# Hybrid encoder trunk on one core: norm-weight waits at first use, one key decay issued earlier, two low parts moved to GpSimd

## The reference, cut to what matters

```
h = rmsnorm(x, norm_mix_pre);  z = h @ w_in
cq, ckv, kr, hq, hff, hfb, hi, hg = split(z)          # 256, 128, 32, then 5 x 512
q  = rmsnorm(cq, q_norm) @ w_uq ; kv = rmsnorm(ckv, kv_norm) @ w_ukv    # 8 heads, 64 + 32 rotary
a  = rmsnorm(softmax attention(q, k, v), att_out_norm)
r  = rmsnorm(gated recurrence forward + backward, hg_out_norm) * silu(hg)   # 4 heads of 128
x  = x + rmsnorm([a, r] @ w_o);  MLP with squared relu;  per-layer embedding gate
```

## Time and profile before

| | |
|---|---|
| median of 3 runs | 1367.94 us |
| the profiled execution | 1365.97 us, of it 1364.2 us from the first to the last instruction |
| mean granted TensorE clock | 0.996 |
| TensorE matmul busy | 1327.0 us, 97% |
| VectorE, ScalarE, GpSimd busy | 877.4, 671.6, 677.9 us |

### The profile page before, as it was taken

The page is one execution under the profiler, slowest core; times in us unless marked ns, Lnnn a source line. Parts: engine busy times, 40 slices in busy tenths (PEclk is TensorE's granted clock), DMA queues, the critical chain, the costliest instruction groups (busy, mean ns, idle before and its releaser), DMA issues.

```text
span 1364.2 us, 22084 instructions
## 1 busy us (share of the span) xinstructions
PE 1327.0 (97%) x8300; PEld 1082.5 (79%) x8300; DVE 877.4 (64%) x1180; ACT 671.6 (49%) x1245; POOL 677.9 (50%) x538
## 2 busy tenths in 40 slices
PE   6999999999989999999999999999999999999997
PEld 5887878877857777888888888888888888878886
DVE  6126656555876775166755565657899888895384
ACT  6333333344458775356755545454544444445452
POOL 4364546365547744455577777775100553003490
PEclk9999999999999999999999999999999999999999
DMA  6231110112240004443533434337667734674351
GB/s 208 70 77 35 30 48 25 36 41 63 55 101 2 1 1 139 170 133 123 194 115 114 126 108 124 111 121 240 231 218 245 245 104 140 236 249 139 87 186 69
DMA packets 138265, 162.28 MB, mean 119 GB/s; under 512 B 16688, under 2 KB 82224, under 8 KB 138160
## 3 DMA queue, kind: packets, MB, share of 16 engines
q1 hardware_dynamic: 138160, 160.87, 37.8%
HBM read 139.86 MB, written 18.87 MB: 116 GB/s over the span
## 4 chain that ended last, share of the span: by engine, by line
PE 78%; DVE 6%; issue 3%; ACT 2%; POOL 2%; DMA 1%; SPq 0%; DVEq 0%; POOLq 0%; ACTq 0%
PE ps L51 23%; PE ps L53 23%; PE ps L52 22%; PE ps L1889 2%; PE ps L1051 2%; PE ps L1930 2%; PE ps L1701 2%; PE ps L1084 1%; DVE op_low L2367 1%; PE ps L998 1%; DVE wy_low L2373 1%; DVE w_sum L2344 0%; DMA gain<-in_att_out_norm 0%; POOL k_low L1718 0%; DMA raw_more<-keep_e 0%
## 5 line engine op out<-in xcount | busy, mean ns | idle before, releaser
L1601 POOL TENSOR_TENSOR wy_low<-w_raw,wy_high 128x512 fp32r<-128x512 f32 x107 | 159.2, 1490 | 179.0 <-ACT wy_high L1544 178.9
L51 PE MATMUL ps<-wy_high,op_high 128*128 128x512 f32 x448 | 175.0, 391 | 1.3 <-DVE wy_low L2373 0.9
L52 PE MATMUL ps<-wy_low,op_high 128*128 128x512 f32 x448 | 174.3, 389 | 0.0
L53 PE MATMUL ps<-wy_high,op_low 128*128 128x512 f32 x448 | 174.3, 389 | 0.0
L1544 ACT ACTIVATE wy_high<-w_raw 128x512 fp32r<-128x512 f32 x118 | 74.4, 631 | 153.7 <-PE ps L53 149.5
L400 POOL TENSOR_TENSOR wx_low<-w_raw,wx_high 128x512 fp32r<-128x512 f32 x62 | 82.8, 1340 | 115.6 <-ACT wx_high L530 115.6
L1601 POOL TENSOR_TENSOR wy_low<-t_sum,wy_high 128x512 fp32r<-128x512 f32 x64 | 89.4, 1397 | 53.9 <-ACT wy_high L1544 53.9
L1544 ACT ACTIVATE wy_high<-w_sum 128x512 fp32r<-128x512 f32 x80 | 50.6, 632 | 119.3 <-PE ps L53 96.5
L1601 POOL TENSOR_TENSOR wy_low<-w_sum,wy_high 128x512 fp32r<-128x512 f32 x32 | 44.5, 1390 | 130.3 <-ACT wy_high L1544 130.3
L51 PE MATMUL ps<-a_high,wy_high 128*128 128x512 f32 x256 | 100.1, 391 | 0.0
L51 PEld LDWEIGHTS ps<-wy_high,op_high 128*128 128x128 f32 x448 | 84.1, 188 | 19.7 <-DVE wy_low L2373 1.7
(11 more groups left out here) (299 smaller groups left out, 3448.0 us busy)
## 6 DMA issues: line engine op xcount, KB each, us to landing
w_raw<-in_w_down SPq DMA_DIRECT2D x127, 256.0 KB, 3.3
raw_more<-in_w_down SPq DMA_DIRECT2D x65, 256.0 KB, 3.5
w_raw<-in_w_up SPq DMA_DIRECT2D x64, 256.0 KB, 3.2
w_raw<-in_w_in SPq DMA_DIRECT2D x62, 256.0 KB, 2.8
w_raw<-in_w_o SPq DMA_DIRECT2D x32, 256.0 KB, 2.9
raw_more<-in_w_up SPq DMA_DIRECT2D x32, 256.0 KB, 3.4
w_raw<-in_w_ple_gate SPq DMA_DIRECT2D x32, 256.0 KB, 2.8
keep_h<-comb SPq DMA_DIRECT2D x26, 256.0 KB, 2.5
```

What stands on the lines that cost most here:

```text
L51: pe.matmul(out, stat_high, mov_high, start=start, stop=False)
L52: pe.matmul(out, stat_high, mov_low, start=False, stop=False)
L53: return pe.matmul(out, stat_low, mov_high, start=False, stop=stop)
L1601: pool.tensor_tensor(low_tile, tile_raw(tile), high_tile.bitcast(F32), ALU.subtract).then_inc(low_made, 1)
```

## The change

Four edits. (1) The wait for the norm weights leaves the head of both attention loops and stands at the first reads: in part 2 of `hgrn_part` and in `norm_scale`. (2) Head 0's level-0 decay of the second group's keys is issued on GpSimd during the last chunk of ("v", 1), ahead of `totals_of(0, 1)`; the slot (lv, 0, 1) issues none any more. (3) The low parts of query latents 2 and 3 (the second half of the tokens) are made by GpSimd behind the query weights' low parts; VectorE makes only the first two. The semaphore `kv_low_made` becomes `pool_low_made` and counts these two and then the two of the key/value latent. (4) The dummy Exp moves from behind the value tile m = 5 to the head of job 12.

```diff
@@ pool_front @@
                     if unit == ("v", 1) and k in (5, 7):
+                        if k == 7:
+                            decay_keys(0, 0)
                         totals_of(0, (k - 5) // 2)
...
-                        if slot[0] == "lv" and slot[2] == 1 and (slot[1] or not j):
+                        if slot[0] == "lv" and slot[2] == 1 and slot[1]:
                             decay_keys(j, slot[1])
...
+                def latent_low(n):
+                    m, h = LAT_PARTS[n]
+                    pool.wait_ge(w_high_made, high_at["lat", n])
+                    pool.tensor_tensor(lat_low[:, m, HALVES[h]], latent[:, m, HALVES[h]],
+                                       lat_high[m][:, HALVES[h]].bitcast(F32), ALU.subtract).then_inc(pool_low_made, 1)
+
                 for k in range(2):
                     latent_weight_low("wq", wq, wq_high, wq_low, k)
+                latent_low(2)
+                latent_low(3)
                 pool.wait_ge(p4_loaded, 16 * 6)
                 pool.wait_ge(rope_step, 1)
...
                 shared_key(0)
-                for h in range(2):
-                    pool.wait_ge(w_high_made, high_at["lat", 4 + h])
-                    pool.tensor_tensor(lat_low[:, 2, HALVES[h]], latent[:, 2, HALVES[h]], lat_high[2][:, HALVES[h]].bitcast(F32),
-                                       ALU.subtract).then_inc(kv_low_made, 1)
+                latent_low(4)
+                latent_low(5)
@@ act_front @@
+                    if n == 12:
+                        act.activation(lb_exp[:, 0:1], minus_half[:, 0:1], ACT.Exp)
...
-                        if m == 5:
-                            act.activation(lb_exp[:, 0:1], minus_half[:, 0:1], ACT.Exp)
@@ dve_front @@
-                                for n in range(4):
+                                for n in range(2):
                                     latent_low(n)
@@ pe_front @@
                     if n < 4:
-                        pe.wait_ge(lat_low_made, 2 * h + 2)
+                        pe.wait_ge(pool_low_made if h else lat_low_made, 2)
                     if n == 12:
-                        pe.wait_ge(kv_low_made, 2)
+                        pe.wait_ge(pool_low_made, 4)
@@ pool_attention, dve_attention @@
                         pool.wait_ge(hg_gated, t + 1)
+                        pool.wait_ge(gains_in, 32)
                         pool.tensor_tensor(tile, tile, gain[:, 0:HH * HK].rearrange("p (h v) -> p h v", h=HH),
                                            ALU.mult).then_inc(hg_done, 1)
...
-                pool.wait_ge(gains_in, 32)
...
                     dve.wait_ge(rstd6_made, t + 1)
+                    dve.wait_ge(gains_in, 32)
...
-                dve.wait_ge(gains_in, 32)
```

More of the change, by code:

```diff
@@ L277, in front_of @@
                      "sig", "lat", "v_act", "v_dve", "z", "hg"))
-            lat_low_made, kv_low_made = sem(top, "p4_lat_low"), sem(top, "p4_kv_low")
+            lat_low_made, pool_low_made = sem(top, "p4_lat_low"), sem(top, "p4_pool_low")
             HIGHS = [("lat", n) for n in range(4)] + [("wq", 0), ("wq", 1), ("lat", 4), ("lat", 5), ("wkv", 0), ("wkv", 1)]
```

## The result

Five runs of each kernel: before 1367.72 us (median; 1364.57 to 1368.2), after 1357.79 us (1356.83 to 1359.61). The ratio is 0.9935 [0.9922, 0.9948] (95% interval), so the change saves 0.65%, 8.9 us by the ratio. I had forecast 1360.5, in a range from 1357.5. The median is inside, but only 0.3 us above the lower edge: the gain is larger than my sum of 6.2.

What follows compares the result with a forecast made beforehand. The prediction took TensorE, busy 97% of the span, as the bound, so only closing its holes or shortening the chain while it waits helps. Terms 3.5 + 1.7 + 1.0 = 6.2 us gave 1360.5 us, range 1357.5 to 1364.5.

Steps and rivals of the forecast that it cites:

- norm-weight waits, with the Exp: Start of attention: first row maximum no longer waits for norm weights, second score pair comes earlier; 3.5 us (2.9 to 3.8).
- head 0's decay: Level 0 of head 0: issuing the decay earlier on GpSimd closes a TensorE wait; 1.7 us (0 to 1.85).
- latents' low parts: Latent jobs: two low parts moved to GpSimd free VectorE by 1.2 us; 1.0 us gained (0.4 to 1.2).
- The first maximum can start at 395.03 instead of 398.79: 3.76 us: Start of attention: without the norm-weight wait, the first row maximum needs only the scores of step 0.
- 4 to 5 us earlier: Sign of being right: the first row maximum of attention starts this much earlier within its own stretch.
- The rival in which another wait takes its place: Start of attention: transfers into `q_t` or the splits replace the norm-weight wait; only 1.7 + 1.0 left, 1364.0 us; 7%.
- Dummy Exp: Moving the table load to job 12 costs nothing and ends TensorE's 0.40 us wait for the last value tile.
- the rival in which the decay brings nothing: Head 0: displaced factor products hold VectorE and then TensorE; 4.5 us gained, 1362.2 us; 10%.
- A gap of about 0.2 us opens and `rot` can pass there: Latent jobs: GpSimd pauses before `wkv_low`, letting VectorE's blocked `rot` product in 3.4 us earlier.
- Most is lost again: Latent jobs: the next `rot` meets GpSimd's run over the shared key, leaving 1.0 us of the gain.
- The rival that VectorE is shut out: Latent jobs: added GpSimd operations pass VectorE's second low part, job 0 starts a microsecond late; 1362.8 us; 15%.
- The rival of exclusion by whole instructions: Latent jobs: no `rot` is held beyond one GpSimd operation; sum 6.4 to 7.5 us, 1359.2 to 1360.3; 10%.

Runs made afterwards that it cites:

- a1: The kernel before with only the norm-weight waits moved to their first reads; 1362.23 us against 1367.07.
- b1: The changed kernel with VectorE making all four latent low parts again; 1358.45 us against 1367.39 for the kernel before.
- a4: The changed kernel with the dummy Exp put back behind the value tile m = 5; 1358.25 us, ratio to the kernel before 0.9939.
- b3: The changed kernel with the shared rotary key added and placed in two token halves, the first before the query results; 1357.57 us, ratio to the kernel before 0.9918.
- c4: The kernel before with GpSimd's first query-result addition also waiting for the key weights' high part, a pause in its run; 1367.9 us in one run.
- a2: The kernel before with only head 0's level-0 decay issued ahead of the factor products; 1363.75 us, ratio 0.9977.
- b2: The kernel before with 34 unread identity products on TensorE behind the score of step 1; 1369.45 us, ratio 1.0017.
- c1: The kernel before with 17 unread identity products on TensorE behind the score of step 1; 1366.41 us against 1368.19.
- c5: The kernel before with three one-column VectorE copies ahead of the second rope shuffle, so `rot` asks later; 1368.99 us against 1368.47.
- a3: The kernel before with only the low parts of query latents 2 and 3 moved to GpSimd; 1366.57 us, ratio 0.9990.
- c3: The changed kernel with the shared key in halves and TensorE's value-tile wait moved behind the score of step 1; 1356.91 us, ratio to the kernel before 0.9923.

## Why the prediction was right, and where its sum was off

| term (us) | forecast | measured |
|---|---|---|
| norm-weight waits, with the Exp | 3.5 | 3.77 |
| head 0's decay | 1.7 | 2.0 |
| latents' low parts | 1.0 | 0.74 |
| TensorE's clock after the hole | none | 1.30 |
| sum | 6.2 | 7.8 |

The measured column is from the stretch table: 6.46 - 2.69, 2.70 - 0.71, (29.70 - 28.97, with rounding) and 19.73 - 18.43. The norm-weight term is known to some 0.3 us, since the waits of like kernels scatter that much. The two profiled executions are 9.2 us apart. Of the 1.4 that the table lacks, about 0.9 lies near 311 us. There the kernel before had a fall of the clock that this profile of after has not. The windows of before, of after, and of after's second profile (c2, first number after the length is TensorE's busy time, then clock, DMA share and GB/s):

```profile
311.50:314.70 3.20, 3.20 (x69) 2.69 (x70) 2.46 (x6) 1.14 (x3) 0.00 (x0) 0.50 0.20 64
```

```profile
308.60:315.20 6.60, 6.60 (x94) 1.00 0.17 51
```

```profile
308.60:315.20 6.60, 6.60 (x81) 0.50 0.19 53
```

c2 is the changed kernel again and has the fall, even a longer one, so this part is chance and no gain. The other 0.5 or so are small steps near 1189 us and at the start, which some kernels show and others don't, whatever their edits.

**Norm-weight waits: right, and a little small.** "The first maximum can start at 395.03 instead of 398.79: 3.76 us" is what a1 shows, 3.77. I had discounted to 3.5 because the second maximum gains less (2.9 to 3.3). The second's smaller gain probably shows one stretch later, as a1's 18.74 beside the 18.44 of b1. The sign "4 to 5 us earlier" doesn't fit this sum of 3.76; after against before shows 3.77. The rival in which another wait takes its place is out.

**Dummy Exp: not additive.** Its place at job 12 costs nothing, as said. Its gain of 0.4 exists only without edit 3; a4 shows zero. What I missed is that with edit 3 the jobs' last product stands 1.9 us ahead of the first score (28.97 - 27.07), so that the load is hidden in either place.

**Decay: right.** I forecast that TensorE's product at 110.06 "comes right behind 107.75 plus 0.46", and it does. The displaced factor products took 4.60 us instead of 3.03, beside VectorE's products of level 0, of which that of the keys took 1.52 us instead of 1.18. The slack ahead of 107.6 covered both, so the rival in which the decay brings nothing is out.

**Latents' low parts: the size near, the way wrong.** VectorE is 1.2 us earlier, as said: `k_swap` starts 0.96 us after job 0 instead of 2.17. Then two steps failed. "A gap of about 0.2 us opens and `rot` can pass there" is wrong: in after no gap opens. GpSimd's addition at 369.24 itself took 1.74 us and `rot` went in at the end of one GpSimd operation. "Most is lost again" is wrong too: no block recurs (1.50, 1.47), and the jobs are 2.3 us shorter, not 1.0. But the reason that I gave for a bound, the transfers of `q_t`, takes back all but 0.74. In before they landed "just ahead of the first score", whose jobs end with this row:

```profile
393.58 0.39 PE L53 MATMUL ps<-wkv_high,lat_low 128*128 128x512 f32 x1
```

Once the jobs ended earlier the transfers came last. Behind the first job, GpSimd's last addition ends only 1.36 us earlier (23.21 to 21.85), and from it to the last landing, behind 1 MB of shared key in the same queue, it takes 0.62 us longer: that leaves 0.74. b3 shows it: with the key placed in halves, the first score comes 1.67 us earlier. So my 1.0 came near by luck, for the gain in the jobs and the loss behind them were both missed.

The rival that VectorE is shut out is false. Its second low part took 2.29 us, as before (2.30), and GpSimd's first added one took 1.72. The rival of exclusion by whole instructions, to which I gave 10%, describes the second to fourth `rot` products of after: each waited for the rest of one GpSimd operation. The Trainium skill (SBUF — State Buffer, Who interferes with whom) says this of any such pair. Seven profiles, those with edit 3 and c4, agree, with 1.44 to 1.51 us. In the other seven (before, a1, a2, b1, b2, c1, c5) the second `rot` took 5.03 to 5.21 us: GpSimd ended the operation that it met, and three more passed it. So that rule doesn't hold in general here. What decides between the two orders stays open.

**The clock: the step that my sum lacked.** I read "0.99" in the window of the hole and didn't look behind it. TensorE came out of the hole at half clock (1.2 instead of 2.4 GHz). The sum put this term at nothing, without a reason. Closing the hole gave back 1.30 us, and filling it alone gave 1.32 (c1). In a1 only 1.0 shows; the other 0.3 is probably the second score pair, which still comes late there. This is the largest error of my sum. Of the 2.7 us by which the median lies below the forecast it accounts for about 1.3; the rest is small errors of the other terms and the scatter of whole runs.

## What to carry to other kernels

A hole in TensorE can cost more than its length: look at the granted clock in the windows behind it, and add what a half-clock stretch there loses. After each part of a change ask which transfer becomes last. Here a queue that was hidden by 0.15 us took two thirds of what a faster VectorE gave, and a large transfer ahead of small ones in one queue was the cause. Terms that lie at one join, as the table load and the shorter jobs, don't add up.

## What the runs showed that I had not expected

- **A fall of the clock after idle time.** All five profiles of kernels with the wait and without fillers (before, a2, a3, c4, c5) have TensorE at half clock from between 395 and 402 us on, right behind or in the hole. None of the other nine has, and among these are both filler kernels, whose hole is at least as long for all other engines. The records give falls of 3.4, 6.8 and 10.2 us, but the stretch lasts 19.71 to 19.74 us in all five, so the recorded length doesn't give the price here, which was 1.3 us.
- **A shorter hole can do it too, now and then.** In b3, c1, c3 and c5 the clock also falls for 3.4 us at 22 us, behind a hole of 1.8 us in TensorE's work, the longest that any profile has there, and their products from there on come about 1.5 us later than in the other ten. In a1 it falls at 110.0 us, behind head 0's hole of 1.86 us, for another 1.6; the six other profiles with that hole don't have it. So edit 2, which closes that hole, may save more than 2.0 us in some executions, which isn't shown.
- **A fall without idle time.** In 11 of 14 profiles, the clock also falls near 310 us, where TensorE is busy throughout (3.20 of 3.20 us above). Kernels that were the same have it in one profile and not in another. By the starts of the same products before and behind it, a fall of 3.4 us costs 0.9 to 1.0 us there and one of 6.8 us 2.4 us, so two profiles can differ by up to 2.4 us for this alone.
- **A blocked operation with two SBUF inputs** took 1.44 to 1.51 us or 5.03 to 5.21 us, nothing between, on the same instruction (the second `rot`) in 14 profiles. What selects between the two is open.
